# First modulation made chunk by chunk, with the input loaded first and four key blocks woven in

## The reference, cut to what matters

```python
mod   = silu(c) @ w_mod + b_mod              # c: (1, 1024), w_mod: (1024, 6144)
mod_c = silu(c_ctx)[None, :] @ w_mod + b_mod # the same weights for the context
sh1, sc1, g1, sh2, sc2, g2 = split(mod, 6)   # likewise for mod_c
h  = rms_norm(x,   norm1_w) * (1 + sc1)  + sh1
hc = rms_norm(ctx, norm1_w) * (1 + sc1c) + sh1c
mk, mq, mv, gates, aq, ak, av, ... = split(h @ w_in)   # likewise from hc
```

## Time and profile before

| | us |
|---|---|
| median of 3 runs | 1287.68 (1286.66 to 1289.17) |
| the profiled execution | 1289.73 |
| its span, first to last instruction | 1287.9 |
| PE busy | 1247.7 (97%) |
| POOL busy | 698.6 (54%) |
| DVE busy | 772.4 (60%) |
| ACT busy | 634.4 (49%) |
| DMA | 208.46 MB, mean 162 GB/s |

### The profile page before, as it was taken

One profiled execution on the slowest core, in us unless ns is written; L12 is line 12 of the kernel. 1 busy time (PEld: TensorE's weight loads), 2 busy tenths in 40 slices (PEclk: granted clock), 3 DMA queues, 4 the chain that ended last, 5 costly groups with the idle time before them and its releaser, 6 DMA issues.

```text
span 1287.9 us, 24946 instructions
## 1 busy us (share of the span) xinstructions
PE 1247.7 (97%) x9287; PEld 1147.4 (89%) x9287; DVE 772.4 (60%) x1435; ACT 634.4 (49%) x1100; POOL 698.6 (54%) x299
## 2 busy tenths in 40 slices
PE   5789999999999999999999999999999999999998
PEld 1588888886789999999988879999999999999998
DVE  3698567636641367677532774677776424677775
ACT  3523233445553565555654645645556446654553
POOL 1445572252237655555858413755565886755564
PEclk8889999999999999999999999999999999999999
DMA  9568662232115534554736312545555664545551
GB/s 374 201 203 311 222 225 74 75 102 79 50 55 171 169 116 179 195 181 172 234 97 191 99 50 66 164 170 188 195 185 175 185 185 156 171 172 179 195 192 70
DMA packets 57740, 208.46 MB, mean 162 GB/s; under 512 B 6576, under 2 KB 7600, under 8 KB 57408
## 3 DMA queue, kind: packets, MB, share of 16 engines
q1 hardware_dynamic: 57168, 205.55, 47.3%
q0 software_dynamic: 496, 1.87, 0.4%
HBM read 206.35 MB, written 1.05 MB: 161 GB/s over the span
## 4 chain that ended last, share of the span: by engine, by line
PE 90%; DVE 5%; DMA 2%; ACT 1%; issue 1%; POOL 0%; SPq 0%; DVEq 0%; ACTq 0%
PE ps L484 24%; PE ps L485 24%; PE ps L486 24%; DMA raw<-in_stream 2%; PE ps L705 2%; PE ps L519 2%; PE ps L522 2%; PE ps L521 2%; PE ps L549 1%; PE ps L772 1%; PE ps L798 1%; PE ps L787 1%; PE ps L925 1%; PE ps L1027 0%; PE ps L637 0%
## 5 line engine op out<-in xcount | busy, mean ns | idle before, releaser
L313 POOL TENSOR_TENSOR wlo<-raw,whi 128x1024 fp32r<-128x1024 f32 x286 | 692.7, 2440 | 551.3 <-ACT whi L1157 526.8
L484 PE MATMUL ps<-Hh,whi 128*128 128x256 f32 (+2 forms) x1976 | 577.0, 292 | 13.1 <-DVE Hl L1646 4.7
L485 PE MATMUL ps<-Hl,whi 128*128 128x256 f32 (+2 forms) x1976 | 568.4, 288 | 0.0
L486 PE MATMUL ps<-Hh,wlo 128*128 128x256 f32 (+2 forms) x1976 | 568.3, 288 | 0.0
L1157 ACT ACTIVATE whi<-raw 128x1024 fp32r<-128x1024 f32 x338 | 352.7, 1052 | 109.1 <-DMA raw<-in_stream 62.5
L484 PEld LDWEIGHTS ps<-Hh,whi 128*128 128x128 f32 (+1 forms) x1976 | 381.4, 193 | 27.9 <-issue 12.7
L485 PEld LDWEIGHTS ps<-Hl,whi 128*128 128x128 f32 (+1 forms) x1976 | 381.6, 193 | 3.2
L486 PEld LDWEIGHTS ps<-Hh,wlo 128*128 128x128 f32 (+1 forms) x1976 | 381.6, 193 | 2.8
L2039 DVE SCALAR_TENSOR_TENSOR arena<-ps,sm,arena 128x255 f32<-128x255 f32 (+1 forms) x264 | 127.3, 483 | 102.7 <-ACT arena L1413 94.7
L484 PE MATMUL ps<-dh,whi 128*128 128x256 f32 x592 | 167.7, 283 | 1.8 <-DVE dl L1951 1.1
L485 PE MATMUL ps<-dl,whi 128*128 128x256 f32 x592 | 167.5, 283 | 0.0
(11 more groups left out here) (314 smaller groups left out, 1218.6 us busy)
## 6 DMA issues: line engine op xcount, KB each, us to landing
raw<-in_stream SPq DMA_DIRECT2D x386, 512.0 KB, 4.1
X<-in_xc SPq DMA_DIRECT2D x2, 1024.0 KB, 10.4
out_y<-X SPq DMA_DIRECT2D x8, 128.0 KB, 2.0
kx<-in_const POOLq DMA_DIRECT2D x1, 512.0 KB, 7.0
arena<-in_wgate POOLq DMA_DIRECT2D x1, 400.0 KB, 8.9
params<-in_params POOLq DMA_DIRECT2D x1, 372.0 KB, 6.9
k<-in_const POOLq DMA_DIRECT2D x1, 256.0 KB, 4.9
kx<-in_const POOLq DMA_DIRECT2D x1, 256.0 KB, 4.6
```

Source lines behind the costliest of these rows:

```text
L313: pool.tensor_tensor(wlo[:, slot, :], raw[:, rslot, :], whi[:, slot, :].bitcast(f32), ALU.subtract).then_inc(rest_done[0], 1)
L484: pe.matmul(out, lh, rh, start=start, stop=False, skip_group_check=True)
L485: pe.matmul(out, lh, rl, start=False, stop=False, skip_group_check=True)
L486: return pe.matmul(out, ll, rh, start=False, stop=stop, skip_group_check=True)
```

## The change

- The first 16 mod blocks are laid out anew: a pair of them now holds all 1024 inputs of 128 outputs of the shift and 128 of the scale, so that chunk k of the modulation is ready behind blocks 2k and 2k+1. Key blocks 0 to 3 are streamed behind the first four pairs.
- X is loaded ahead of the stream, in four quarters. Constants and parameters are cut in an early and a late part; the late parts and the rotary constants are issued by POOL after the sixteenth mod block has been used. The gate weights come as 16 columns and are put in place on the chip.
- PE, chunk by chunk: products of the next chunk's modulation, gates, key block 0, the turning of the next chunk's modulation (two products with a selector), then parts of key blocks 1 to 3 from a list. Each key block has its own bank (0 to 3), the gates bank 4.
- DVE, chunk by chunk: the two full-precision halves, the copy of the next modulation, the two differences, the finish of the next modulation. Six of the eight normed chunks move to POOL, between the first four rests.
- ACT makes the log-sigmoid's functions ahead of evac(0) and evac(1).

```diff
+N_MK = W_IN_JOBS.index("mq")
+STREAM = []
+for _k in range(KC):
+    STREAM += [("mod", 2 * _k), ("mod", 2 * _k + 1)]
+    STREAM += [("w", _k)] if _k < N_MK else []
 _n = MOD_FIRST
-for _s in range(S_BRANCH):
+for _s in range(N_MK, S_BRANCH):
...
             sp.dma_start(c_raw, ccol_d).then_inc(s_ccol, 16)
-            load(0)
-            load(1)
-            for half in range(2):
-                sp.dma_start(X[:, 4 * half:4 * half + 4, :], xc_d[:, 4 * half:4 * half + 4, :])\
-                  .then_inc(s_x[half], 16)
-            r = 2
+            for i in range(4):
+                sp.dma_start(X[:, 2 * i:2 * i + 2, :], xc_d[:, 2 * i:2 * i + 2, :]).then_inc(s_x[i], 16)
+            r = 0
...
-            pool.dma_start(K0[:, :], const_d).then_inc(s_k0, 16)
-            pool.dma_start(PR[:, :], params_d).then_inc(s_par, 16)
-            pool.dma_start(ar(A_KT, KC * GATE_P), wgate_d).then_inc(s_wg, 16)
-            pool.wait_ge(mod_used, 9)
-            pool.dma_start(KX[:, :], const1_d).then_inc(s_kx, 16)
+            pool.dma_start(K0[:, 0:C_MASKA], const_d[:, 0:C_MASKA]).then_inc(s_k0, 16)
+            pool.dma_start(wg_cols, wgate_d).then_inc(s_wg, 16)
+            pool.dma_start(PR[:, 0:P_EARLY], params_d[:, 0:P_EARLY]).then_inc(s_par, 16)
+            pool.memset(wg_raw, 0.0).then_inc(S["wg_clear"], 1)
...
+            def x_unit(k):
+
+                pool.tensor_tensor(sq[:, k, :], X[:, k, :], n_r, ALU.mult).then_inc(S["x_unit_pool"], 1)
+
+            pool.wait_ge(S["x_unit"], 2)
+            rest(0)
+            x_unit(2)
+            x_unit(3)
+            rest(1)
+            x_unit(4)
+            rest(2)
+            rest(3)
+            for k in (5, 6, 7):
+                x_unit(k)
+            pool.wait_ge(mod_used, MOD_FIRST)
+            pool.dma_start(K0[:, C_MASKA:C_KEEP], const_d[:, C_MASKA:C_KEEP]).then_inc(s_k0b, 16)
+            pool.dma_start(PR[:, P_EARLY:N_PARAMS], params_d[:, P_EARLY:N_PARAMS]).then_inc(s_par2, 16)
+            pool.dma_start(KX[:, :], const1_d).then_inc(s_kx, 16)
+
+            s = N_MK
...
+                bank = q if kind == "mk" else 0 if kind in ("mo", "gm") else len(_own) % 2
...
+            def mod_products(k):
+
+                if k >= 2:
+                    pe.wait_ge(S["mod_ready"], k - 1)
+                for h in range(2):
+                    n = 2 * k + h
+                    wait_raw(pe, RAW_OF_MOD[n])
+                    for j in range(4):
+                        mm = pe.matmul(PS[32 * j:32 * j + 32, 6 + k % 2, 0:256], c_cols[:, 4 * h + j, :],
+                                       raw[:, RAW_OF_MOD[n] % RING, 256 * j:256 * j + 256], start=h == 0, stop=h == 1)
+                    mm.then_inc(mod_used, 1)
+
+            def mod_turn(k):
+
+                pe.wait_ge(S["mod_copy"], k + 1)
+                for s in range(2):
+                    mm = pe.matmul(PS[:, 6 + k % 2, 256 + 2 * s:258 + 2 * s], mod_rows[k % 2][:, P * s:P * s + P], selv,
+                                   start=True, stop=True)
+                mm.then_inc(S["mod_t"], 1)
+
+            def gates(k):
+
+                pe.wait_ge(S["wg_lo"], 1)
                 pe.wait_ge(S["hl_done"], 2 * k + 2)
-                mm = mm3(PS[0:GATE_P, 2, :], wgh[:, k, :], wgl[:, k, :], Hh[:, k, :], Hl[:, k, :],
-                         k == 0, k == KC - 1)
+                mm = mm3(PS[0:GATE_P, 4, :], wgh[:, k, :], wgl[:, k, :], Hh[:, k, :], Hl[:, k, :], k == 0, k == KC - 1)
                 if k == KC - 1:
                     mm.then_inc(S["gates_ps"], 1)
-                for q in range(2):
-                    mm = mm3(PS[:, q, :], *w(q, k), Hh[:, k, :], Hl[:, k, :], k == 0, k == KC - 1)
-                    if k == KC - 1:
-                        mm.then_inc(blk_done, 1)
+
+            def key_part(q, k):
+
+                wait_rest(pe, q)
+                if q >= 2 and k == 0:
+                    pe.wait_ge(S["c_across"], 1)
+                mm = mm3(PS[:, q, :], *w(q, k), Hh[:, k, :], Hl[:, k, :], k == 0, k == KC - 1)
+                if k == KC - 1:
+                    mm.then_inc(blk_done, 1)
+
+            KEY_PARTS = [[], [(1, 0), (1, 1)], [(1, 2), (2, 0), (2, 1), (2, 2)],
+                         [(1, 3), (2, 3), (3, 0), (3, 1), (3, 2), (3, 3)]]
+            KEY_PARTS += [[(q, k) for q in range(1, N_MK)] for k in range(4, KC)]
+
+            pe.wait_ge(S["silu_c"], 1)
+            pe.wait_ge(s_k0, 16)
+            for c in range(KC):
+                mm = pe.matmul(PS[:, 2 + c // 4, P * (c % 4):P * (c % 4) + P],
+                               c_cols[:, c, 0:1].broadcast_to((P, P)), ident, start=True, stop=True)
+            mm.then_inc(S["c_bc"], 1)
+            pe.wait_ge(S["sq_sum"], KC - 1)
+            pe.matmul(PS[:, 1, :], ones, sq[:, 0, :], start=True, stop=True).then_inc(S["ss_ready"], 1)
+            mod_products(0)
+            mod_turn(0)
+            for k in range(KC):
+                if k + 1 < KC:
+                    mod_products(k + 1)
+                gates(k)
+                key_part(0, k)
+                if k + 1 < KC:
+                    mod_turn(k + 1)
+                for part in KEY_PARTS[k]:
+                    key_part(*part)
...
+            for q in range(N_MK, 28):
+                if q == MV_ONES_AT:
+                    pe.wait_ge(S["gate_add"], 1)
+                gp_job(q)
...
+            for d in range(2):
+                for g in range(2):
+                    at = 64 * g + 32 * d
+                    act.activation(wg_raw.rearrange("p (k n) -> p k n", k=KC)[:, :, at:at + 4],
+                                   wg_cols.rearrange("p (k n) -> p k n", k=KC)[:, :, 8 * d + 4 * g:8 * d + 4 * g + 4],
+                                   ACT.Copy).then_inc(S["wg_put"], 1)
+            act.wait_ge(S["wg_put"], 4)
...
+            SPLITS_BEHIND = {0: 1, 2: 3, 6: 4}
+            splits_upto(0)
+            for k in range(KC):
+                act.wait_ge(S["mod_ready"], k + 1)
+                act.wait_ge(*((S["x_unit"], k + 1) if k < 2 else (S["x_unit_pool"], k - 1)))
+                for v in range(2):
+                    u = 2 * k + v
+                    act.activation(Hh[:, k, v * T:v * T + T], sq[:, k, v * T:v * T + T], ACT.Identity,
+                                   bias=MOD[:, k, 0, v:v + 1], scale=SC[:, u:u + 1]).then_inc(S["hh_done"], 1)
+                if k in SPLITS_BEHIND:
+                    splits_upto(SPLITS_BEHIND[k])
...
-                    if q == 0:
-                        act.wait_ge(S["wg_lo"], 1)
...
-            evac(0)
-            evac(1)
...
             for q in range(28):
-                if q >= 2:
-                    evac(q)
+                evac(q)
...
+            def mod_copy(k):
+
+                dve.wait_ge(mod_used, 2 * k + 2)
+                dve.tensor_copy(mod_rows[k % 2], PS[:, 6 + k % 2, 0:256]).then_inc(S["mod_copy"], 1)
+
+            def mod_finish(k):
+
+                dve.wait_ge(S["mod_t"], k + 1)
+                ps = PS[:, 6 + k % 2, 256:260]
+                link(dve.tensor_scalar(MOD[:, k, 0, :], ps[:, 0:2], pr("b_mod", 2 * k, 2 * k + 1), None, ALU.add))
+                dve.tensor_scalar(SC[:, 2 * k:2 * k + 2], ps[:, 2:4], b_scale[:, k:k + 1], pr("norm1", k, k + 1),
+                                  ALU.add, ALU.mult).then_inc(S["mod_ready"], 1)
...
+                for k in range(2):
+                    dve.tensor_tensor(sq[:, k, :], X[:, k, :], n_r, ALU.mult).then_inc(S["x_unit"], 1)
+                    if k == 0:
+                        mod_copy(0)
+                mod_finish(0)
                 for k in range(KC):
-                    dve.tensor_tensor(sq[:, k, :], X[:, k, :], n_r, ALU.mult).then_inc(S["x_unit"], 1)
-                dve.wait_ge(s_par, 16)
-                mod_finish()
-                for u in range(2 * KC + 1):
-                    if u < 2 * KC:
-                        k, v = divmod(u, 2)
-                        if v == 0:
-                            dve.wait_ge(S["x_unit"], k + 1)
+                    dve.wait_ge(S["mod_ready"], k + 1)
+                    dve.wait_ge(*((S["x_unit"], k + 1) if k < 2 else (S["x_unit_pool"], k - 1)))
+                    for v in range(2):
+                        u = 2 * k + v
                         if u >= 2:
                             dve.wait_ge(S["hl_done"], u - 1)
-                        dve.tensor_scalar(PS[:, 5, T * (u % 2):T * (u % 2) + T], sq[:, k, v * T:v * T + T],
+                        dve.tensor_scalar(PS[:, 5, T * v:T * v + T], sq[:, k, v * T:v * T + T],
                                           SC[:, u:u + 1], MOD[:, k, 0, v:v + 1], ALU.mult, ALU.add)\
                            .then_inc(S["h32_done"], 1)
-                    if u >= 1:
-                        k, v = divmod(u - 1, 2)
-                        dve.wait_ge(S["hh_done"], u)
-                        dve.wait_ge(S["h32_done"], u)
```

(48 more changed lines are left out.)

57 lines of the change are left out of this document (15 added, 42 removed).

## The result

The changed kernel takes 1308.12 us (median of 4 runs, 1304.26 to 1312.73) beside 1288.15 of the kernel before: ratio 1.0151, interval [1.0129, 1.0173]. Timed again beside the experiments it took 1304.86 (1303.91 to 1305.33), ratio 1.0119 [1.0103, 1.0134]; that is the base for them. Forecast were 1290.9 and a range up to 1296.5: the sign was right, a rise of 3.2 us was forecast and one of 16 to 20 was measured. The profiled execution took 1304.26, span 1302.5 (before 1287.9): 14.6 us.

The account below looks back on a forecast made before the run. Query block 6's start on PE was taken as the bound: G at 62.9 plus 21.3 gives 84.2 instead of 81.05, +3.2 us, so 1287.68 + 3.2 = 1290.9. Range for eight in ten: 1282.5 to 1296.5.

Parts of the forecast that it names:

- What bounds the kernel: Start: only the moment query block 6 starts on PE counts, 81.05 us before; PE has work without a gap from there.
- G: End of the gate sum on DVE, which starts the chain to query block 6: 59.2 us before, 62.9 forecast.
- 1, the opening: From the start to the first chunk: additions of squares end at 11.6, first `Hl` at 21.9 us instead of 40.2.
- 2, the loop: Loop over chunks: circles of 4.8 us, longer at chunks 2 and 3; last `Hl` at 59.5 instead of 52.9.
- the clock's share: Loop over chunks: PE's low clock at the start adds 1.2 us in all, or 8 if it lasts three circles.
- the 0.8 that step 2 holds out for four groups: Loop's mod products: if four column groups halve the measured pair's price for a block, G comes 0.8 us earlier.
- 3, from the last `Hl` to G: DVE waits 0.6 us for late parameters, then gains, mod 16 and gate sum: G at 62.9 us.
- 4, from G to block 6: Gate chain: functions start earlier, but POOL's rests draw out the scans; 21.3 us instead of 21.8.
- The faster ones: Rivals: PE's own order ends last, 1278.9 us, or short loop with both turns saved, 1283.9; together chance 0.21.
- that of no difference: Rival: one turn less or a quicker loop, so G's loss and the earlier functions cancel: 1287.7 us, chance 0.28.
- The clock rival: Much slower: PE's short bursts keep the low clock for three circles or more, 6.8 us more: 1297.7, chance 0.08.
- the rule that step 2 cites: Loop's mod products: the Trainium skill says products in different column groups of the array run at the same time.

Follow-up runs that it names:

- e3: The kernel before, with evacuations of query blocks 1 to 3 on ACT put ahead of w 9's split: 1288.85 us, ratio 0.9995.
- e5: The changed kernel with early parameters awaited behind the additions of squares and POOL's rest of the gate weights made after them: 1302.04 us, ratio 1.0093.
- e1: The changed kernel with DVE's copy of the next chunk's modulation moved behind the two differences: 1297.66 us, ratio 1.0061.
- e6: The changed kernel with the log-sigmoid's three functions back behind evac(0) and evac(1): 1305.51 us, ratio 1.0133.
- e2: The changed kernel with all parts of key blocks 1 to 3 put behind the last chunk: 1297.59 us, ratio 1.0061.
- e12: The changed kernel with e1, e5, evacuations as in e3, exponentials behind evac(6), late parameters after 12 mod blocks, two parts a circle from chunk 1: 1281.16 us, ratio 0.9940.
- e11: The kernel before with e3's order, exponentials behind evac(6), and late parameters and rotary constants issued after the sixteenth mod block: 1281.73 us, ratio 0.9941.

## Why the prediction was wrong

- **What bounds the kernel.** Right as to place: query block 6, G and the chain behind it. The growth of the span (14.6) is the shift of that moment (14.0). Incomplete: it took the moment for the only one, and e3 shows a second wait on the same chain.
- **1, the opening.** First `Hl` 25.9 instead of 21.9, +4.0. The step that failed is "they begin with the first quarter of X, about 6.1, and end at 11.6". I had put the added waits at nothing because they end "before 12, beside the squares and additions". The wait for the early parameters stands ahead of the additions and ended at 8.6, and the rest of the gate weights on POOL falls on the last addition. Without both (e5) the additions end at 12.8; the 1.2 left over the forecast are mostly a wait of 0.95 for the squares on ACT and a later first one (6.54 for 6.1). From the end of the additions on, the step came out right: 10.1 us against 10.3 forecast.
- **2, the loop.** The step that failed: "In the 2.9 that PE waits for DVE in it, it has to do the parts of key blocks 1 to 3 and the next mod products". DVE's own order has the copy, which needs these products, ahead of the differences. PE's parts and mod products must be over when DVE has done the finish and the halves, 1.6 us behind the turn (62.15 to 63.71), not after 2.9 (the prediction's own terms, 4.8 less 1.38 and 0.66, give 2.8), and then copy and differences (1.1) and the hand-over follow. A circle is then gates and key block 0, turn, parts, mod products, copy, differences one after the other; for chunk 5 that is 1.6 + 0.34 + 2.2 + 1.04 + 0.34 + 0.75 + 0.15 = 6.4, and 6.5 were measured. Seven circles took 7.3 more than forecast. The copy's waits are 10.3, of which the forecast had 2.8 as parts that are too long, so 7.5 are new, and e1 gave 7.5 of last `Hl` back (some of it from the clock in circle 0). I had listed the copy's price and not its wait. Smaller terms: mod products 1.04 a chunk for 0.9, and the clock's share 1.6 (circle 0) for 1.2. The 0.45 a block was misread as the price with two column groups; it is that of four (last section), so the 0.8 that step 2 holds out for four groups was not there to gain.
- **3, from the last `Hl` to G.** 3.7 for 3.35. The late parameters landed 6.4 behind the sixteenth mod product, 5.1 were worked out, and cost 1.0 for 0.6.
- **4, from G to block 6.** 20.5 for 21.3, with the three turns of DVE and POOL in the forecast order. e6 confirms the exchange.
- **The sum.** 4.0 + 7.3 + 0.4 on G, less 0.8, makes 10.9 of the 10.8 by which block 6 came later than forecast (95.04 for 84.2).
- **The rivals.** The faster ones and that of no difference all took circles of about 4.8 or less for granted; the clock did not decide here but in e2's profile. The clock rival's "0.45 of work every 1.28" is misread: PE was busy without a pause from 15.2 to 20.1 us (L562, sixteen products in 4.89 us), in which the clock rose. The range ended at 1296.5 because no rival was a longer circle at the full clock.

## What to carry to other kernels

When work is woven into a loop that two engines close together, write each engine's order down for one round and mark what every instruction waits for: the price of an instruction in such a circle is its wait, which everything queued behind it shares, not its own length. A copy that serves the next round belongs behind this round's results. Then fill the waiting engine only as far as its pause goes (two parts here): more lengthens the round, and with no parts in it e2's profile had granted clocks of 0.50 to 0.70 for 30 us. And when one wait on a chain is taken off, look for the next on the same chain (e3, e12).

## What the runs showed of the hardware

Four column groups work side by side, and the kernel before used them already: its blocks lie in groups 0 and 1 and in groups 2 and 3 in turn (`j = 2 * s + half`, L562). A block that came alone took 1.05 us, four that were waiting took 2.35, 0.59 each, as two ran at once. Each further one took 0.43, (2.35 - 1.05)/3, and this is step 2's 0.45.

```profile
33.14 1.05 PE L562 MATMUL ps<-raw,arena 128*32 128x512 f32 x4 [0.23 <-DMA raw<-in_stream]
```

```profile
57.79 1.07 PE L589 MATMUL ps<-raw,arena 128*32 128x256 f32 x16
```

The second line is the changed kernel's: two blocks, each spread over all four groups, in 1.07, 0.54 each. For blocks that wait the new layout brings next to nothing, and nothing here speaks against the rule that step 2 cites; it was applied to the wrong price.

An operation of DVE with two operands in SBUF is held for whole instructions of POOL, whatever its own size: 128x16 elements took 3.61 us in e11, 4x256 took 2.76.

28 KB over POOL's queue took about as long (6.1 us) as 512 KB of X over SP's (median 6.4) at the start, so here the small transfer was not an early one.
